# One weight split moved forward in two places, one square added on TensorE instead of GpSimd, and ten unused products in front of two products that wait for h

## What is computed

```python
    x = x + rms_norm(merged @ w_out[l], g[1])
    h = rms_norm(x, g[2])
    x = x + rms_norm(memory_cross_attention(h, mem_n, xa_wq[l], xa_wkv[l], xa_wo[l]), g[3])
    h = rms_norm(x, g[4])
    x = x + rms_norm(conv_glu_ffn(h, ffn_up[l], ffn_conv[l], ffn_down[l]), g[5])
...
    hn = rms_norm_2(h, attn_norm[l])
    proj = hn @ w_in[l]
```

## Time and profile before

| | us |
|---|---|
| median of 3 runs | 1907.52 |
| lowest and highest of them | 1906.23, 1907.6 |
| the profiled execution | 1915.01 |
| its span, first to last instruction | 1913.2 |
| TensorE busy in the span | 1821.0 |
| VectorE, ScalarE, GpSimd busy | 1018.1, 732.8, 295.6 |

### The profile page before, as it was taken

The page is one execution under the profiler, slowest core; times in us unless marked ns, Lnnn a source line. Parts: engine busy times, 40 slices in busy tenths (PEclk is TensorE's granted clock), DMA queues, the critical chain, the costliest instruction groups (busy, mean ns, idle before and its releaser), DMA issues.

```text
span 1913.2 us, 22240 instructions
## 1 busy us (share of the span) xinstructions
PE 1821.0 (95%) x8975; PEld 1460.5 (76%) x8975; DVE 1018.1 (53%) x1518; ACT 732.8 (38%) x1220; POOL 295.6 (15%) x236
## 2 busy tenths in 40 slices
PE   7899999999999988989999999899878999999998
PEld 5778876788888876778888788787656788888887
DVE  6777845444454466357777722574365534444422
ACT  4433344332334444344444422445456532222221
POOL 2013501011212040141111100500100101111100
PEclk9999999999999989999999999898978899999999
DMA  5222322233224421222232233221201122222321
GB/s 188 88 77 89 110 82 79 72 112 98 91 96 157 141 86 36 68 76 88 88 103 96 74 103 99 97 102 63 97 25 32 49 95 92 96 95 93 99 89 56
DMA packets 49829, 171.13 MB, mean 89 GB/s; under 512 B 5882, under 2 KB 8570, under 8 KB 49600
## 3 DMA queue, kind: packets, MB, share of 16 engines
q1 hardware_dynamic: 45216, 155.69, 24.7%
q0 software_dynamic: 3936, 13.51, 2.1%
q10 hardware_dynamic: 576, 0.52, 0.1%
HBM read 165.51 MB, written 4.19 MB: 89 GB/s over the span
## 4 chain that ended last, share of the span: by engine, by line
PE 81%; DVE 7%; ACT 5%; issue 4%; POOL 2%; DMA 0%; SPq 0%; DVEq 0%; POOLq 0%; ACTq 0%
PE ps L377 25%; PE ps L379 25%; PE ps L378 25%; PE ps L382 3%; PE ps L2588 2%; ACT ws_h L305 1%; DVE ws_l L313 1%; POOL sums L424 1%; ACT P L2712 1%; PE ps L2605 1%; POOL x L1433 1%; DMA x<-in_x 0%; DVE tmp L807 0%; DVE mg_l L873 0%; PE ps L2600 0%
## 5 line engine op out<-in xcount | busy, mean ns | idle before, releaser
L313 DVE TENSOR_TENSOR ws_l<-raw,ws_h 128x1024 fp32r<-128x1024 f32 x289 | 394.1, 1369 | 529.0 <-ACT ws_h L305 528.6
L377 PE MATMUL ps<-h_h,ws_h 128*128 128x512 f32 (+1 forms) x1448 | 584.5, 404 | 20.8 <-DVE h_l L540 9.7
L378 PE MATMUL ps<-h_l,ws_h 128*128 128x512 f32 (+1 forms) x1448 | 572.9, 396 | 0.0
L379 PE MATMUL ps<-h_h,ws_l 128*128 128x512 f32 (+1 forms) x1448 | 572.6, 395 | 0.0
L305 ACT ACTIVATE ws_h<-raw 128x1024 fp32r<-128x1024 f32 x289 | 303.3, 1054 | 453.6 <-PE ps L379 448.7
L377 PEld LDWEIGHTS ps<-h_h,ws_h 128*128 128x128 f32 x1448 | 278.0, 192 | 94.9 <-issue 16.1
L379 PEld LDWEIGHTS ps<-h_h,ws_l 128*128 128x128 f32 x1448 | 278.4, 192 | 62.0
L378 PEld LDWEIGHTS ps<-h_l,ws_h 128*128 128x128 f32 x1448 | 279.7, 193 | 58.5
L377 PE MATMUL ps<-G_h,ws_h 128*128 128x512 f32 (+1 forms) x374 | 143.7, 384 | 3.9 <-DVE ws_l L313 3.9
L379 PE MATMUL ps<-G_h,ws_l 128*128 128x512 f32 (+1 forms) x374 | 143.1, 383 | 0.0
L378 PE MATMUL ps<-G_l,ws_h 128*128 128x512 f32 (+1 forms) x374 | 143.1, 383 | 0.0
(11 more groups left out here) (435 smaller groups left out, 2421.9 us busy)
## 6 DMA issues: line engine op xcount, KB each, us to landing
raw<-in_ffn_up SPq DMA_DIRECT2D x88, 512.0 KB, 3.3
raw<-in_w_merge SPq DMA_DIRECT2D x36, 512.0 KB, 3.3
raw<-in_ffn_down SPq DMA_DIRECT2D x22, 512.0 KB, 3.4
raw<-in_w_down SPq DMA_DIRECT2D x22, 512.0 KB, 3.3
raw<-in_w_hy SPq DMA_DIRECT2D x12, 512.0 KB, 3.9
raw<-in_w_sc SPq DMA_DIRECT2D x12, 512.0 KB, 3.4
raw<-in_fwd SPq DMA_DIRECT2D x8, 512.0 KB, 3.4
raw<-in_w_naqk SPq DMA_DIRECT2D x8, 512.0 KB, 3.3
```

Source lines behind the costliest of these rows:

```text
L313: dve.e.tensor_tensor(w.lo, raw[n % NRAW][:], w.hi, ALU.subtract).then_inc(*lo_made.says(("lo", n)))
L377: pe.e.matmul(o, a.hi, b.hi, start=start, stop=False, skip_group_check=True)
L378: pe.e.matmul(o, a.hi, b.lo, start=False, stop=False, skip_group_check=True)
L379: return pe.e.matmul(o, a.lo, b.hi, start=False, stop=stop, skip_group_check=True)
```

## The change

Four edits:

- `added_tiles`: in passage n2 GpSimd adds the squares of tiles 1 to 5 only. The square of tile 6 is added by TensorE itself in `total_of_tokens`, with four more 128x1 instructions that read it where ScalarE wrote it.
- `XA_BESIDE` has 4 and 6 in the place of 5, and the loops behind it in `xa_act` and `xa_dve` make one call less.
- In `ffn1_act` and `ffn1_dve` the down projection's next eight blocks are called in step 22 before `finish(20)` and `finish(21)`.
- `keep_warm`: ten products 128x512 of operands that lie in SBUF, without a use of their result, in front of the first product of n4 and of n6. They go into the bank that this first product then starts anew.

```diff
     def total_of_tokens(v, o, of=4, part=0):
 
         ats = [128 * (of * part + j) for j in range(of)]
-        pe.wait_ge(("added", key(v), 6))
+        pe.wait_ge(("added", key(v), added_tiles(v)))
         for j, at in enumerate(ats):
             mm32(o[:, j:j + 1], acc[:, at:at + 128], ones[:, 0:1], j == 0, False)
+        for m in range(added_tiles(v) + 1, 7):
+            pe.wait_ge(("sq", v, m))
+            for j, at in enumerate(ats):
+                mm32(o[:, j:j + 1], T[place.get(("sq", v, m), 0)][:, at:at + 128], ones[:, 0:1], False, False)
         pe.wait_ge(("sq", v, 7))
...
+    def added_tiles(v):
+
+        return 5 if v == "n2" else 6
...
+    def keep_warm(o, a, b):
+
+        for _ in range(10):
+            pe.e.matmul(o, a, b, start=True, stop=True, skip_group_check=True)
...
     def squares_pool(v):
-        for m in range(1, 7):
+        for m in range(1, added_tiles(v) + 1):
...
-    XA_BESIDE = (1, 2, 3, 5)
+    XA_BESIDE = (1, 2, 3, 4, 6)
...
         for m in range(5):
-            if m:
+            if m > 1:
                 f.next(8)
...
             o = bank(first[t], main) if k == 0 else out_of(first[t])
+            if v == "n4" and t == k == 0:
+                keep_warm(o, XQ[:, 7, 0:128].hi, XQ[:, 0, :].hi)
             pe.wait_ge(("h", v, k))
...
+                if n == 22:
+                    down.next(8)
                 if i:
                     finish(i - 1)
         finish(21)
...
-            down.next((36, 0)[m] if m < 2 else 22)
+            down.next((28, 0)[m] if m < 2 else 22)
...
                 o[t] = [bank(("cq", t), main)] if t < 2 else [bank(("kv", i), main) for i in range(2)]
+                if t == 0:
+                    keep_warm(o[t][0], G1[:, 21, 0:128].hi, G1[:, 0, :].hi)
             pe.wait_ge(("h", "n6", k))
```

## The result

| | before | after |
|---|---|---|
| median of 12 runs each, one comparison | 1910.09 us (1906.23 to 1916.66) | 1905.79 us (1903.21 to 1909.45) |
| profiled execution, and its span | 1915.01, 1913.2 us | 1908.49, 1906.7 us |
| mean granted clock of TensorE in it | 0.971 | 0.974 |

The ratio is 0.9976, 95% interval 0.9965 to 0.9988: 4.6 us faster, between 2.3 and 6.7. The forecast was 7.3 us off and 1900.2; the time lies 1.9 us outside the range.

The account below looks back on a forecast made before the run. The prediction took TensorE's work plus its waits to bound the kernel. Its terms, 4.5 + 2.5 + 0.3 = 7.3 us, taken off the median of 1907.52, gave 1900.2 us, with a range of 1899 to 1902.5.

Parts of the forecast that it names:

- What bounds the kernel: Whole kernel: TensorE, busy 1821.0 of 1913.2 us; an edit pays only where it shortens TensorE's work or its waits.
- Down projection, 4.5: Third chunk's earlier split removes a 2.99 us wait and 1.49 us of slow products behind it; bounds 3.0 and 5.5.
- rival 4: Down projection: the split waits at its new place for data or buffer; about 1905 us, chance 0.07 with the rest.
- n2, 2.5: Passage n2: products resume 2.0 us earlier, plus 0.5 of the slow stretch; bounds 0.3 and 5.4.
- the start of the total: In n2, TensorE's total of the squares was to start at 698.3 instead of 700.62, a wait of 0.7 us.
- h tile 3's lo: In n2, VectorE was to finish it at 684.6, 0.2 us before TensorE's fourth block: no wait.
- rival 1: The wait passes on to h or the next chunk in n2 or the down projection: 1902.7 to 1904.2 us, chance 0.20.
- The ten products, 0.3: In front of n4 and n6: hidden; 0 in n4, 0.3 us taken for both; bounds 0 and 2.2.
- Rival 2: The ten products in n4 and n6 keep the clock high: 9.5 to 12 us gained, 1895.5 to 1898, chance 0.15.
- Rival 3: Clock fall put off behind h tile 3 in blocks 3 to 7 of n4 and n6: slower, 1909.2 us, chance 0.03.
- The sum, 7.3: Whole kernel: 4.5 us in the down projection, 2.5 in n2 and 0.3 for the ten products.
- The time, 1900.2: Whole kernel: 7.3 us taken off the runs' median of 1907.52; range 1899 to 1902.5, chance 0.55.

Follow-up runs that it names:

- e3_warm: The kernel before plus only the ten unused products in front of n4 and n6, against the kernel before: 1909.05 us, ratio 0.9987.
- f3_only_n4: The whole change with the ten products in n4 only, not in n6, against the kernel before: 1898.60 us, ratio 0.9949.
- e2_n2: The kernel before plus only the two n2 edits (square of tile 6 on TensorE, split one tile earlier), against the kernel before: 1906.71 us, ratio 0.9975.
- g1_whole: The changed kernel with nothing edited, measured a third time, against the kernel before: 1904.66 us, ratio 0.9958.
- e4_nowarm: The whole change without the ten products in n4 and n6, first measurement, against the kernel before: 1902.16 us, ratio 0.9946.
- f2_nowarm: The whole change without the ten products in n4 and n6, second measurement, against the kernel before: 1901.60 us, ratio 0.9954.
- g2_nowarm: The whole change without the ten products in n4 and n6, third measurement, against the kernel before: 1902.74 us, ratio 0.9952.

## Why the prediction was right or wrong

- **What bounds the kernel**: right. Both gains came from TensorE's waits and the slow products behind them.
- **Down projection, 4.5**: right, in place, in both halves (2.98 and 1.49) and by itself on the chip (5.2, interval 2.3 to 7.8). The lo took 1.22 us as in the better case, and rival 4 did not occur.
- **n2, 2.5**: the mechanism right, the size short. The step that was mis-sized is the start of the total, 2.3 us earlier by the forecast (698.3 for 700.62) and 2.9 by the traces, counted from the spread. Two things make up the difference: the squares begin 0.7 us earlier, the upper end of the 0.1 to 0.7 that I gave, where I used 0.4; and the addition left out was worth 2.19 us (10.75 less 8.56), where I took a mean one of 1.79. Then the 24 records took 2.67 us where 2.85 was forecast, so products resume 2.75 earlier instead of 2.0. Of the slow stretch 0.8 came back in the changed kernel's profile (0.5 forecast) and 2.4 in two others; my estimate over all profiles is 3.4 for the term. Alone it measured 4.8 (2.7 to 6.9). The term's bounds don't follow from their own stamps: 703.16 less 702.7 is 0.5 and not 0.3, and 24 records at the 2.85 of the term end at 700.45 and not at 700.2, which makes 5.2 of 5.4. The moved split's lo took the 2.32 us that I priced it with. h tile 3's lo was forecast for 684.6, and is done at 684.2; TensorE, 1.7 us early there, most of it by its clock (0.53 from 681.0 to 684.6 before), waits 1.12 us for it. So the part of rival 1 that I saw 0.2 us away did come into play, without a loss against before.
- **The ten products, 0.3**: right, and for the reason given. n4 is paced by h; n6 had up to 1.1 us to give, only in the runs whose fall reached furthest into the passage. Rival 2 (they keep the clock high) is right about the clock and wrong about the time. Rival 3 occurred in part: twice the fall was put off until h tile 0 had come, in n6 of e3_warm (0.50 from 1214.6 to 1217.8) and in n4 of f3_only_n4 (0.50 from 823.9 to 827.2). Both times it was over before the fourth block, at 1220.6 and 829.9, and TensorE caught up with h; behind the fourth block no clock of 0.50 stands.
- **The sum, 7.3**: the three comparisons gave 4.6, 8.2 and 8.0 us, 6.2 weighted, with 7.3 within the interval of two of them and outside the first by 0.6.
- **The time, 1900.2: wrong.** The step that failed is the last: the sum was taken off the median of three runs, 1907.52. The kernel before has its median at 1910.1 to 1912.1 in the larger sets, and single runs from 1903.5 to 1919.1. I noted that the profiled run lay 7.5 us over that median and could name no reason; the likely one is that both were draws from one wide spread, for 1907.5 and 1915.0 both lie within it. From 1910.09 the same sum gives 1902.8, inside my range, and the measured 1905.79 is 3.0 from it. Of the 5.6 us missed, 2.6 are the anchor, 3.0 what the changed kernel came out short of the sum in the first comparison; by the slope above its lower clock could be the larger part of these, which is not shown. The range was built from the terms alone, and had no part for the anchor.

The version to keep is the change without the ten products: 0.9946, 0.9954 and 0.9952, no slower than the changed kernel in either shared comparison, with less code, though not measurably faster than it there.

## What to carry to other kernels

A wait is worth itself plus the slow products behind it only where nothing else paces the engine afterwards. Before you price a clock gain, look for the next wait: behind a producer that delivers at its own pace, a faster TensorE only waits longer, and a mean clock that rises does not show that time was gained. Count a stage from its own first instruction, not from the start of the span: what was won or lost ahead of it otherwise shows up as its gain. And treat the anchor as a term with an error of its own: with three runs shown and a profiled run 7 us away from them, the spread between runs belongs into the range.

## What was not expected of the hardware

- The mean rate of a dense stream has two values. The same two products of the FFN's first half, 861 starts apart, in before and after:

```profile
870.08 0.40 PE L379 MATMUL ps<-h_h,ws_l 128*128 128x512 f32 x1
...
1070.20 0.39 PE L379 MATMUL ps<-h_h,ws_l 128*128 128x512 f32 x1
```

```profile
868.01 0.40 PE L379 MATMUL ps<-h_h,ws_l 128*128 128x512 f32 x1
...
1068.99 0.40 PE L379 MATMUL ps<-h_h,ws_l 128*128 128x512 f32 x1
```

  200.12 and 200.98 us, both at clock 1.00: from start to start 0.2324 or 0.2334 us in the mean. Eight of the fourteen profiles have the first value in this stretch and six the second, and one and the same kernel has both (e4_nowarm the first, f2_nowarm and g2_nowarm the second). It costs 0.9 us, and its cause stays open.
- Of a VectorE and a GpSimd instruction that overlap, the one that began first kept its time here, and the later one took longer. In the down projection VectorE's lo of the split began at 1091.49 and took 1.22 us, and GpSimd's product, from 1091.72, took 2.14 instead of 1.61; VectorE's next one, begun beside that product, took 1.78 instead of 0.69. In n2 the lo that began beside an addition of GpSimd already running since 680.08 took 2.32 (row at 680.59).
- The slow stretch behind a wait may come or not. With the same edits in n2 and the same starts of the total to within 0.4 us, e2_n2 ran on at full clock and the changed kernel did not (from 701.75 to 704.73 its products start 0.43 us apart). One and the same kernel does both: g1_whole is the changed kernel too, and its clock is 1.00 from 696 to 720 us.
